# Cached key pages turned by VectorE in 32x32 blocks, and their scores as sixteen 32x32 tiles

## The chip, the cores and the metric

The kernel runs on one core of a Trainium2 chip. The metric is the device time of one execution in microseconds (us): the median of three runs.

## The reference

One inference step of a small two-layer decoder: 256 prompt tokens and 64 sample tokens (8 sequences of 8 new tokens), model width 1024. The first layer is a retention layer, then keys and values shared by the rest are computed, and the second layer is attention with 8 heads of width 128. For the sample tokens, attention also reads a paged cache: 8 sequences, 2 pages each, a page being 128 positions x 8 heads x 128. What the change touches is this part:

```
def moba_sample(q, k_new, v_new, cache_k, cache_v, page_table, rel_bias):
    ...
        k_past = cache_k[pages].reshape(past, MOBA_HEADS, MOBA_HD)
...
    s_sel = jnp.einsum('qhd,qhjld->qhjl', q, k_sel).astype(jnp.float32) + b_sel
...
    p = jax.nn.softmax(logits, axis=-1)
```

So for each sequence and head, 8 queries meet 256 cached keys over a width of 128, in float32, a bias is added, and a softmax over the cached and the own keys follows.

## The kernel before

Each engine has one in-order program, written out from a single list of steps that `make_schedule` (L128) lays down; the engines meet at semaphores only. TensorE's main work is the projections: a weight matrix is streamed in chunks of 1 MB. For each chunk the steps WS split it on ScalarE (`w_hi`, L1185) and VectorE (`w_lo`, L1523) into two parts, in four pieces, and TensorE makes three products per block (L881, L884, L865). Small steps of attention are hung between the tiles of a chunk, at numbered slots: six slots to a chunk of three tiles, one in the middle and one at the end of each tile.

The stretch that matters holds five such chunks. I call them K1, K2, K3, K4 (key projection: the two halves of the depth for the first 512 columns, then for the second) and V1 (the first half of the first value projection). Their slots are 0 to 29. After each tile of K2 and K4 the key rows are complete, and the step TILE normalises them: square on ScalarE (L1357), sum on VectorE (L1683), root on ScalarE (L1359), reciprocal (L1686) and four scalings on VectorE (L1692). The third tile first adds two halves (L1549).

Cached keys, before: SyncE loads page n (`load_page`, L665) into one of four buffers `cache`, 128 positions on the partitions. Step KP n turns it: eight 128x128 transposes on TensorE (L1048) into two PSUM banks, copied out to `ktc` by VectorE (L1815) and ScalarE (L1453). Step KS b (L1061), for one sequence, multiplies the two turned pages with that sequence's queries: eight matmuls 128x32 by 256, four of them in different column groups of the array, all into bank 5. The queries lie spread over zeros in `wide`, written by ScalarE in step ME (L1251). Step SE (L1824) adds the bias for the first four sequences, and step SA p does it for the others and takes the maximum (L1837 to L1850). KX turns the new keys (L1077), SN scores them (L1092), SB turns the weights of the softmax, PV multiplies them with value pages.

```
    for n in range(8):
        at = 2 + 3 * n
        if n:
            g[at].append(("KS", n - 1))
        if n == 4:
            g[at].append(("SE",))
        g[at] += [("KP", 2 * n), ("KP", 2 * n + 1)]
```

Each of VectorE, ScalarE, GpSimd and SyncE walks through the same list, so within a slot the order is: split pieces, then the steps of the middle slot, then TILE, then the steps of the end slot.

Of the kernel before, what the change touches and what calls it, by code (L numbers as in the profile page):

```python
# [33 lines left out]
P = 128  # L34
D = 1024
# [38 lines left out]
def shape_constants():  # L74
# [21 lines left out]
    own = np.arange(P)[:, None] % 32 // NEW == np.arange(4)[None, :]  # L96
# [11 lines left out]
def kp_banks(n):  # L108

    return (6, 7) if n % 2 else (3, 4)  # L110
# [17 lines left out]
def make_schedule():  # L128
# [48 lines left out]
    def add(*s):  # L177
# [4 lines left out]
        if s[0] == "KS" and s[1] % 4 == 0:  # L182
            fill(5, "PS", s[1] // 4)
        if s[0] == "KP":
            for b in kp_banks(s[1]):
                fill(b, *s)
# [61 lines left out]
    for n in range(8):  # L248
        at = 2 + 3 * n
        if n:  # L250
            g[at].append(("KS", n - 1))
        if n == 4:
            g[at].append(("SE",))
# [42 lines left out]
def build(nc, a):  # L296
# [3 lines left out]
    with ctx:  # L300
# [109 lines left out]
        spread = wide.ap().rearrange("p n (b x) -> p n b x", x=32)[:, :, :, 0:NEW]  # L410
# [3 lines left out]
        yf = flat_ktc[:, :, 2 * (TP + P):D]  # L414
        flat_sqs = mvp[:, 0, 0:4 * P]
        sqs = flat_sqs.rearrange("p (g h m) -> p g h m", g=2, m=32)
# [55 lines left out]
        wide_cleared, pads_cleared = sem("wide_cleared"), sem("pads_cleared")  # L472
        q_sq_done = sem("q_sq_done")
# [45 lines left out]
        def await_ks(eng, n):  # L519

            b = n // 2
            if n < 0:
                return
            if b % 4 == 3:
                await_full(eng, 5, "PS", b // 4)
            else:
                eng.wait_ge(ks_done, b + 1 - (b + 1) // 4)

        def window(n, bb):

            return wide[:, n, 24 * bb:24 * bb + 32]

# [90 lines left out]
        def _(sp):  # L623
# [41 lines left out]
            def load_page(n):  # L665

                m, vals = n % 16, n >= 16
# [5 lines left out]
                src = a["cache_v"] if vals else a["cache_k"]  # L673
                sp.dma_start(cache[:, n % NCP, :], src[bass.ds(page, 1)].rearrange("o p h d -> p (o h d)"))\
                    .then_inc(cache_loaded[n % NCP], 16)
# [19 lines left out]
            for step in steps:  # L695
# [74 lines left out]
                elif kind == "ME" and step[1] == 5:  # L770
                    sp.wait_ge(lines_stored, 64)
                    for h in range(MH):
                        r0 = 32 * (h % 4)
                        sp.dma_start(bs[r0:r0 + 32, h // 4, :],
                                     bass.AP(scratch.tensor, h * LINE + FAR - PAST, [[0, 4], [skew, NEW], [1, PAST + NEW]]))\
                            .then_inc(bias_loaded, 16)
# [34 lines left out]
        def _(pe):  # L811
# [83 lines left out]
            for step in steps:  # L895
# [145 lines left out]
                elif kind == "KP":  # L1041
                    n = step[1]
                    pe.wait_ge(cache_loaded[n % NCP], 16 * (n // NCP + 1))
                    for h in range(MH):
                        b = kp_banks(n)[h // 4]
                        if h % 4 == 0:
                            await_free(pe, b, *step)
                        mm = pe.transpose(bank[b][:, P * (h % 4):P * (h % 4) + P], cache[:, n % NCP, P * h:P * h + P], ident)  # L1048
                        if h % 4 == 3:
                            close(mm, b)  # L1050
                elif kind == "KS":
                    b = step[1]
                    for n in range(2 * b, 2 * b + 2):
                        for kp_bank in kp_banks(n):
                            await_read(pe, kp_bank, "KP", n)
# [954 lines left out]
```

## Time and profile before

| | before |
|---|---|
| median of 3 runs, us | 509.81 |
| lowest, highest | 509.31, 509.97 |
| span of the profiled execution, us | 508.2 |
| TensorE busy | 502.0 us, 99% |
| VectorE busy | 352.5 us, 69% |
| ScalarE busy | 263.2 us, 52% |
| GpSimd busy | 74.6 us, 15% |
| DMA | 125.49 MB, mean 247 GB/s |

The span runs from the first to the last instruction of one profiled execution. The profile states no total time for it besides the span; the median of the runs is 1.6 us above it. Busy shares are averages over the whole span; TensorE's matmuls are pipelined, so 99% says that it hardly waits, not that it works at its peak.

### The profile page before, as it was taken

To read this page: it belongs to the slowest core of one execution; us is meant where nothing else is said; L and a number is where in the kernel's file an instruction comes from. 1 tells how busy PE (TensorE), PEld (TensorE's weight loads), DVE (VectorE), ACT (ScalarE), POOL (GpSimd) and SP (SyncE) were. 2 spreads that over 40 slices of the span, in tenths; PEclk is the share of its full clock that TensorE was granted. 3 is DMA by queue.
4 is the path that set the end of the run, shared out by engine and by line. 5 is a ranking of instruction groups with operands and counts; after the bars stand their busy time and mean duration, and the time that the engine had idled before them with its cause. 6 is when DMAs were issued, how large, how long until landed. Compare 5 with 4: busy or idle time off the path is not lost.

```text
span 508.2 us, 9171 instructions
## 1 busy us (share of the span) xinstructions
PE 502.0 (99%) x3401; PEld 434.0 (85%) x3401; DVE 352.5 (69%) x651; ACT 263.2 (52%) x532; POOL 74.6 (15%) x85
## 2 busy tenths in 40 slices
PE   7999999999999999999999999999999999999997
PEld 6989978899779978898899999977877778999885
DVE  3865539884789829893598978836756765676662
ACT  5836532574428633464652556945444655655630
POOL 0291004520082102720000240000000000000000
PEclk9999999999999999999999999999999999999999
DMA  8993969999899898999937976526797657684211
GB/s 256 333 349 118 275 245 313 376 358 231 284 343 386 235 277 283 354 328 230 264 103 277 334 244 256 188 83 238 249 326 238 216 171 242 226 309 154 83 53 52
DMA packets 79375, 125.49 MB, mean 247 GB/s; under 512 B 4051, under 2 KB 42148, under 8 KB 79204
## 3 DMA queue, kind: packets, MB, share of 16 engines
q1 hardware_dynamic: 79250, 124.89, 75.4%
q8 instruction: 27, 0.44, 0.4%
q14 instruction: 16, 0.13, 0.1%
q10 hardware_dynamic: 82, 0.02, 0.0%
HBM read 98.93 MB, written 27.57 MB: 249 GB/s over the span
## 4 chain that ended last, share of the span: by engine, by line
PE 95%; DVE 2%; DMA 1%; ACT 1%; issue 1%; SPq 0%; DVEq 0%; ACTq 0%
PE bank L884 45%; PE bank L881 20%; PE bank L865 7%; PE bank L1048 3%; PE bank L993 3%; PE bank L1061 2%; PE bank L1115 1%; PE bank L1007 1%; PE bank L940 1%; PE bank L1161 1%; PE bank L820 1%; PE bank L973 1%; PE bank L974 1%; PE bank L975 1%; DMA eye<-in_c_eye 1%; PE bank L961 1%
## 5 line engine op out<-in xcount | busy, mean ns | idle before, releaser
L1523 DVE TENSOR_TENSOR w_lo<-w_raw,w_hi 128x512 fp32r<-128x512 f32 x207 | 143.8, 733 | 65.7 <-ACT w_hi L1185 65.2
L1185 ACT ACTIVATE w_hi<-w_raw 128x512 fp32r<-128x512 f32 x208 | 118.4, 620 | 58.3 <-PE bank L884 35.0
L884 PE MATMUL bank<-xn_hi,w_hi 128*128 128x320 f32 x320 | 100.1, 317 | 0.7 <-ACT w_hi L1185 0.7
L884 PE MATMUL bank<-xn_hi,w_lo 128*128 128x320 f32 x320 | 97.7, 309 | 0.1
L884 PE MATMUL bank<-xn_lo,w_hi 128*128 128x320 f32 x320 | 97.6, 309 | 0.0
L881 PE MATMUL bank<-w_hi,xn_hi 128*128 128x512 f32 x160 | 65.0, 406 | 0.0
L884 PEld LDWEIGHTS bank<-xn_hi,w_hi 128*128 128x128 f32 x320 | 59.7, 188 | 4.7 <-issue 2.9
L881 PE MATMUL bank<-w_lo,xn_hi 128*128 128x512 f32 x160 | 62.6, 391 | 0.0
L881 PE MATMUL bank<-w_hi,xn_lo 128*128 128x512 f32 x160 | 62.5, 390 | 0.0
L884 PE MATMUL bank<-ym_hi,w_hi 128*128 128x320 f32 x192 | 60.9, 317 | 0.0
L884 PEld LDWEIGHTS bank<-xn_lo,w_hi 128*128 128x128 f32 x320 | 59.8, 188 | 0.4 <-DVE xn_lo L1572 0.2
L884 PEld LDWEIGHTS bank<-xn_hi,w_lo 128*128 128x128 f32 x320 | 59.7, 188 | 0.3 <-DVE w_lo L1523 0.3
L884 PE MATMUL bank<-ym_hi,w_lo 128*128 128x320 f32 x192 | 59.3, 309 | 0.0
L884 PE MATMUL bank<-ym_lo,w_hi 128*128 128x320 f32 x192 | 59.3, 309 | 0.0
L1745 DVE SCALAR_TENSOR_TENSOR st<-st,bank 128x512 f32<-128x512 f32 x64 | 39.6, 680 | 6.2 <-PE bank L1007 6.2
L884 PEld LDWEIGHTS bank<-ym_hi,w_hi 128*128 128x128 f32 x192 | 36.1, 188 | 1.8 <-issue 1.7
L884 PEld LDWEIGHTS bank<-ym_lo,w_hi 128*128 128x128 f32 x192 | 36.1, 188 | 0.1
L881 PEld LDWEIGHTS bank<-w_hi,xn_hi 128*128 128x128 f32 x160 | 30.1, 188 | 7.2 <-issue 1.7
L884 PEld LDWEIGHTS bank<-ym_hi,w_lo 128*128 128x128 f32 x192 | 36.0, 188 | 0.0
L881 PEld LDWEIGHTS bank<-w_lo,xn_hi 128*128 128x128 f32 x160 | 30.0, 188 | 6.6
L881 PEld LDWEIGHTS bank<-w_hi,xn_lo 128*128 128x128 f32 x160 | 30.1, 188 | 5.4
L1941 POOL TENSOR_TENSOR fin<-raw_qk,cst 128x320 f32<-128x320 f32 x16 | 17.4, 1111 | 108.4 <-DMA out_ret_state_prompt<-fin 67.2
(265 smaller groups left out, 766.5 us busy)
## 6 DMA issues: line engine op xcount, KB each, us to landing
w_raw<-in_ret_w_in SPq DMA_DIRECT2D x23, 1024.0 KB, 10.8
st<-in_state_ret SPq DMA_DIRECT2D x32, 512.0 KB, 8.4
out_ret_state_sample<-st SPq DMA_DIRECT2D x32, 512.0 KB, 4.6
w_raw<-in_ret_w_out SPq DMA_DIRECT2D x8, 1024.0 KB, 8.8
w_raw<-in_moba_w_in SPq DMA_DIRECT2D x8, 1024.0 KB, 6.1
cache<-in_cache_k SPq DMA_DIRECT2D x16, 512.0 KB, 4.9
w_raw<-in_w_kv SPq DMA_DIRECT2D x8, 1024.0 KB, 6.4
cache<-in_cache_v SPq DMA_DIRECT2D x16, 512.0 KB, 4.0
```

The source lines that it names most:

```text
L820: mm = pe.transpose(bank[kt][:, c0:c0 + m], st[0:m, t, P * kt:P * kt + P], ident[0:m, 0:m])
L865: mm = pe.matmul(bank[b][:, :], xn_hi[:, k, TP:T + TS], w[:, wk, :], start=k == 0 and n == 0, stop=k == KT - 1 and n == 1)
L881: mm = pe.matmul(bank[b][0:m, :], x[:, k, c0:c0 + m], w[:, wk, :], **flags)
L884: mm = pe.matmul(bank[out][:, 0:T], w[:, wk, P * tile:P * tile + P], x[:, k, :], **flags)
L940: mm = pe.matmul(bank[5][0:m, col:col + n], kT[:, d, j:j + m], qT[:, d, i0:i0 + n], start=d == 0, stop=d == 1)
L993: mm = pe.matmul(bank[5][32 * j:32 * j + 32, :], qz[:, q0:q0 + 32], st[:, b, DV * d:DV * d + DV], start=False, stop=g == 1 and d == 1, ski ...
L1048: mm = pe.transpose(bank[b][:, P * (h % 4):P * (h % 4) + P], cache[:, n % NCP, P * h:P * h + P], ident)
L1061: mm = pe.matmul(bank[5][32 * j:32 * j + 32, PAST * half_at:PAST * half_at + PAST], window(2 * h + b // 4, b % 4), ktc[:, :, h, :], start= ...
L1185: act.activation(w_hi[:, c % 2, part], w_raw[:, c % RAW, part], ACT.Copy).then_inc(w_hi_done, 1)
L1523: dve.tensor_tensor(w_lo[:, c % 2, part], w_raw[:, c % RAW, part], w_hi[:, c % 2, part].bitcast(F32), ALU.subtract).then_inc(w_lo_done, 1)
L1745: dve.scalar_tensor_tensor(state, state, math.exp(NEW * LOG_DECAY[h]), bank[up_bank(b, d)][:, :], ALU.mult, ALU.add).then_inc(bank_read[up ...
L1941: done(pool.tensor_tensor(to, x, tab, ALU.mult))
```

## The change

- Key pages are loaded in another layout. Partition group g (32 partitions) of the page buffer holds heads 2g and 2g+1, with position 32c+i of the page on partition i of the group. That takes four DMAs to a page with runs of 256 numbers, in place of one with runs of 1024. The pages come in another order (`key_page`), four to a quad: two sequences.
- KP n is one VectorE instruction: it turns 32 blocks of 32x32 in each group of partitions (1024 elements on each partition), SBUF to SBUF, into `ktc` or the new `ktc2`. These two hold one quad; the next quad waits for the scores of the last. No TensorE or ScalarE work is left in KP.
- KS q, now four steps, multiplies a quad: 64 matmuls of a 32x32 tile of the array by 256 columns, over four blocks e of the head width, four partition groups (each into its own bank, 3 to 6) and four column groups. KP 0 to 15 stand in slots 0-3, 6-9, 12-15 and 18-21, KS 0 to 3 in slots 5, 11, 17 and 23.
- SE has two steps (slots 12 and 24), each with four instructions, since a score is now the sum of two banks. The instruction L1837 in SA falls away.
- `wide` is filled by GpSimd in ME, four small copies to a head, where ScalarE's one instruction (L1251) falls away. GpSimd also builds `own_q`, and clears part of `wide` after the last KS.
- SN has twice as many matmuls, and KX turns 128 rows where the last tile had 64. KX 0 and 1 move to slots 14 and 16. The bias loads are sixteen DMAs in place of eight.

```diff
+def key_page(n):
+
+    q, s, pg = n // 4, n % 4 // 2, n % 2
+    return NPG * (4 * (q // 2) + 2 * s + q % 2) + pg
...
-    for n in range(8):
-        at = 2 + 3 * n
...
-        g[at] += [("KP", 2 * n), ("KP", 2 * n + 1)]
-    g[16].append(("KX", 0))
-    g[18].append(("KX", 1))
-    g[26].append(("KS", 7))
+    for n, at in enumerate((0, 1, 2, 3, 6, 7, 8, 9, 12, 13, 14, 15, 18, 19, 20, 21)):
+        g[at].append(("KP", n))
+    for q, at in enumerate((5, 11, 17, 23)):
+        g[at].append(("KS", q))
+    g[12].append(("SE", 0))
+    g[24].append(("SE", 1))
+    g[14].append(("KX", 0))
+    g[16].append(("KX", 1))
...
                 elif n >= NCP:
-                    await_full(sp, kp_banks(n - NCP)[1], "KP", n - NCP)
+                    sp.wait_ge(kt_done, n - NCP + 1)
...
+                src = a["cache_k"][bass.ds(page, 1)].rearrange("o (c i) h d -> i (o c) (h d)", i=32)
+                for g in range(4):
+                    sp.dma_start(cache[32 * g:32 * g + 32, n % NCP, :].rearrange("p (c x) -> p c x", c=4), src[:, :, 256 * g:256 * g + 256])\
+                        .then_inc(cache_loaded[n % NCP], 16)
...
                 elif kind == "KS":
...
+                    q = step[1]
+                    pe.wait_ge(kt_done, 4 * q + 4)
+                    pe.wait_ge(wide_filled, MH)
+                    if q % 2 == 0:
+                        for b in PS_BANKS:
+                            await_free(pe, b, "PS", q // 2)
+                    last = {}
+                    for e in range(4):
+                        for s in range(2):
+                            at = 32 * (2 * s + q % 2) - NEW * (q % 2)
+                            for h in range(2):
+                                for g in range(4):
+                                    rows_at, c0 = slice(32 * g, 32 * g + 32), 32 * (2 * h + s)
+                                    keys_of = (ktc, ktc2)[s][rows_at, :, 4 * h + e, :]
+                                    last[g] = pe.matmul(bank[PS_BANKS[g]][c0:c0 + 32, 0:PAST], wide[rows_at, 8 * h + 2 * e + q // 2, at:at + 32],
+                                                        keys_of, start=q % 2 == 0 and e == 0, stop=q % 2 == 1 and e == 3,
+                                                        skip_group_check=True)
...
                 elif kind == "KP":
                     n = step[1]
-                    b = kp_banks(n)[0]
-                    await_full(dve, b, *step)
-                    await_ks(dve, n - 2)
-                    dve.tensor_copy(ktc[:, n % 2, 0:4, :], bank[b][:, :].rearrange("p (h k) -> p h k", h=4))\
-                        .then_inc(bank_read[b], 1)
+                    dve.wait_ge(cache_loaded[n % NCP], page_loaded(n))
+                    if n >= 4:
+                        await_ks(dve, n // 4 - 1)
+                    dve.transpose(keys_turned(n), cache[:, n % NCP, :].rearrange("p (c x j) -> p x c j", c=4, j=32)).then_inc(kt_done, 1)
...
                 elif kind == "SE":
...
+                    for x in range(2):
+                        for u in range(2):
+                            b, p = PS_BANKS[2 * u + x], 2 * half + u
+                            to = scores_at(p)[:, 0:PAST]
+                            dve.scalar_tensor_tensor(to, bank[b][:, 0:PAST], rsq[:, 16 + p:17 + p], to if x else bs[:, u, 0:PAST],
+                                                     ALU.mult, ALU.add).then_inc(bank_read[b], 1)
...
+            def spread_queries(h):
+
+                g, x = h // 2, h // 2 % 2
+                pool.wait_ge(q_done, h + 1)
+                for e in range(4):
+                    done.wait()
+                    ins = pool.tensor_copy(slots[32 * g:32 * g + 32, 8 * (h % 2) + 2 * e:8 * (h % 2) + 2 * e + 2, :, 16 * x:16 * x + NEW],
+                                           mqT[32 * e:32 * e + 32, h, TP:T].rearrange("p (n b t) -> p n b t", n=2, t=NEW))
```

## Rows read from the trace of the kernel before

**Rows 1.** The profile's page: busy time and share, and the clock by slices.

```profile
PE 502.0 (99%) x3401; PEld 434.0 (85%) x3401; DVE 352.5 (69%) x651; ACT 263.2 (52%) x532; POOL 74.6 (15%) x85
PEclk9999999999999999999999999999999999999999
```

**Rows 2.** The page's chain that ended last, by engine.

```profile
PE 95%; DVE 2%; DMA 1%; ACT 1%; issue 1%; SPq 0%; DVEq 0%; ACTq 0%
```

**Rows 3.** The chain in order of time, 334 to 396 us: start, length, what.

```profile
335.30 1.75 PE bank L1048 x16
...
341.60 1.00 PE bank L1061 x16
342.60 1.90 PE bank L1048 x16
344.50 4.11 PE bank L881 x18
...
390.93 0.85 PE bank L1077 x6
...
395.22 0.63 PE bank L1092 x32
```

**Rows 4.** Busy time by stretch: length; PE, PEld, DVE, ACT, POOL; clock, DMA share, GB/s.

```profile
335.10:395.20 60.10, 60.10 (x442) 45.51 (x444) 36.24 (x78) 27.73 (x56) 0.00 (x0) 1.00 0.72 246
```

**Rows 5.** VectorE's groups in that stretch: busy us, mean ns, idle before.

```profile
L1523 DVE TENSOR_TENSOR w_lo<-w_raw,w_hi 128x512 fp32r<-128x512 f32 x17 | 11.1, 683 | 6.0 <-ACT w_hi L1185 6.0
L1815 DVE COPY ktc<-bank 128x512 f32<-128x512 f32 x16 | 10.5, 682 | 4.5 <-PE bank L1048 4.3
```

**Rows 6.** VectorE's timeline: start us, us, instruction, and the idle time before.

```profile
345.69 1.29 DVE L1523 TENSOR_TENSOR w_lo<-w_raw,w_hi 128x512 fp32r<-128x512 f32 x2 [0.90 <-ACT w_hi L1185]
348.00 0.69 DVE L1683 TENSOR_REDUCE small<-scr 128x4 f32<-128x512 f32 x1 [1.02 <-ACT scr L1357]
349.27 1.13 DVE L1692 SCALAR_TENSOR_TENSOR rows<-bank,small,knw 128x128 f32<-128x128 f32 x4
350.31 0.68 DVE L1523 TENSOR_TENSOR w_lo<-w_raw,w_hi 128x512 fp32r<-128x512 f32 x1
...
356.48 0.67 DVE L1549 TENSOR_TENSOR rows<-bank,rows 64x512 f32<-64x512 f32 x1
357.85 0.68 DVE L1683 TENSOR_REDUCE small<-scr 64x4 f32<-64x512 f32 x1 [0.70 <-ACT scr L1357]
363.16 0.86 DVE L1824 SCALAR_TENSOR_TENSOR ps<-bank,small,bs 128x256 f32<-128x256 f32 x2
```

**Rows 7.** VectorE's groups of other shapes, whole execution; L1760: min/median/max ns.

```profile
L1787 DVE TENSOR_TENSOR scr<-scr,rsb 128x1280 f32<-128x1280 f32 x3 | 4.5, 1488 | 0.1
L1874 DVE TENSOR_SCALAR ktc<-ktc,small 128x256 f32<-128x256 f32 x8 | 2.8, 353 | 0.3
L1875 DVE TENSOR_SCALAR ktc<-ktc,small 128x128 f32<-128x128 f32 x8 | 2.2, 279 | 0.0
L1692 DVE SCALAR_TENSOR_TENSOR rows<-bank,small,knw 128x128 f32<-128x128 f32 x16 | 4.5, 344 | 0.1
L1760 DVE TENSOR_TENSOR scr<-scr x4: 825/1472/1483, 94.3 to 253.3; 128x640 f32<-128x640 f32 x4
```

**Rows 8.** TensorE's tiled matmuls in time: start us, us.

```profile
348.55 1.07 PE L1061 MATMUL bank<-ktc,wide 128*32 128x256 f32 x16
83.03 0.50 PE L1007 MATMUL bank<-vq,kq 32*128 32x512 f32 x4
395.15 0.65 PE L1092 MATMUL bank<-mkT,mqT 128*32 128x64 f32 x32
```

**Rows 9.** SyncE's DMA issues in time: start us, us of issuing, transfer.

```profile
366.04 0.55 SPq L789 DMA_DIRECT2D out_k_sample<-rows  x1
371.57 0.35 SPq L674 DMA_DIRECT2D cache<-in_cache_k  x1
```

**Rows 10.** GpSimd's group of 64-column operations: busy us, mean ns, idle before.

```profile
L1954 POOL TENSOR_TENSOR qz<-qT,cst 128x64 f32<-128x64 f32 x8 | 6.0, 760 | 0.0
```

More of the change, by code:

```diff
@@ L181, in add @@
             fill(5, "UR", s[1])
[L182 to L186, printed above, removed]
+        if s[0] == "KS" and s[1] % 2 == 0:
+            for b in PS_BANKS:
+                fill(b, "PS", s[1] // 2)
         if s[0] == "SB":
@@ L1040, in _ @@
                     close(mm, 7)
[L1041 to L1050, printed above, removed]
-                elif kind == "KS":
[L1052 to L1055, printed above, removed]
-                    if b % 4 == 0:
-                        await_free(pe, 5, "PS", b // 4)
-                    for half_at in range(2):
-                        for j in range(4):
-                            h = 4 * half_at + j
-                            mm = pe.matmul(bank[5][32 * j:32 * j + 32, PAST * half_at:PAST * half_at + PAST],
-                                           window(2 * h + b // 4, b % 4), ktc[:, :, h, :],
-                                           start=b % 4 == 0 and half_at == 0, stop=b % 4 == 3 and half_at == 1,
-                                           skip_group_check=True)
-                    if b % 4 == 3:
-                        close(mm, 5)
@@ L1067, in _ @@
                     else:
[L1068 removed]
+                        last[3].then_inc(ks_done, 1)
                 elif kind == "KX":
@@ L1073, in key_columns @@
                     def key_columns(i, t):
-                        c0, m = TOK[t]
+                        c0 = TOK[t][0]
                         at = 256 * (c % 2) + P * i
-                        return pe.transpose(bank[6 + i][:, c0:c0 + m], rows[0:m, t, at:at + P], ident[0:m, 0:m])
+                        return pe.transpose(bank[6 + i][:, c0:c0 + P], rows[:, t, at:at + P], ident)
+                    if c == 0:
+                        pe.wait_ge(pads_cleared, 1)
                     for i in range(2):
@@ L1820, in _ @@
                 elif kind == "SE":
-                    await_full(dve, 5, "PS", 0)
-                    dve.wait_ge(bias_loaded, 16 * MH)
-                    for u in range(2):
-                        ins = dve.scalar_tensor_tensor(ps[:, u, 0:PAST], bank[5][:, PAST * u:PAST * u + PAST],
-                                                       rsq[:, 16 + u:17 + u], bs[:, u, 0:PAST], ALU.mult, ALU.add)
-                    ins.then_inc(bank_read[5], 1)
+                    half = step[1]
+                    dve.wait_ge(bias_loaded, 32 * MH)
+                    for b in PS_BANKS:
+                        await_full(dve, b, "PS", half)
+                    for x in range(2):
+                        for u in range(2):
[3 more added lines that the diff above has]
+                                                     ALU.mult, ALU.add).then_inc(bank_read[b], 1)
+                        if x == 0:
+                            await_read(dve, PS_BANKS[0], "PS", half)
+                            await_read(dve, PS_BANKS[2], "PS", half)
                 elif kind == "SA":
```

147 lines of the change are left out of this document (83 added, 64 removed).

## The prediction

> **What bounds the kernel now.** I read the page first: TensorE is busy 99% of the span, at the full clock in every slice [rows 1], and the chain that ended last is 95% TensorE [rows 2]. So work taken from TensorE shortens the run, as long as the engine that takes it over keeps up. The chain in order of time shows what goes: eight blocks of sixteen page transposes between the projections' matmuls, 1.75 us the first and 1.90 us the others, and eight score blocks of 1.00 us [rows 3]. The busy times of this stretch, 335.1 to 395.2 us, show who has room: VectorE is busy 36.24 of 60.10 us, ScalarE 27.73, GpSimd not at all [rows 4]. VectorE's groups say what it does there, and its timeline in which order, which is what will count [rows 5, 6].
>
> **TensorE's own sum.** The transposes fall away: 1.75 + 7 x 1.90 = 15.05 us. Score blocks: a block before has 16 instructions of 256 columns, four column groups side by side, in 1.00 us [rows 3, 8]: four rounds of 0.215 us (256 columns, two cycles each at 2.4 GHz) and 0.14 us of entry and exit. Four row groups have run side by side too: four matmuls of 512 columns have starts within 0.01 us and all end within 0.50 us [rows 8]. Rows and columns split at once are in no row. At best sixteen tiles share a round: the 128 instructions of a quad take 8 x 0.215 + 0.14 = 1.86 us, say 1.9. At worst only four run at a time: 32 rounds, 7.0 us. Between these, the 32 small instructions of SN start within 0.58 us, so issuing one takes at most 18 ns [rows 8]; by that bound alone a block is 2.3 us. I take 1.9, since both splits alone have run at full width, and keep 7.0. So scores cost 4 x 1.9 = 7.6 us where they cost 8.0; SN doubles from 0.63 us [rows 3] to 1.3; KX stays near 0.75 a step (0.85 in its row [rows 3]). TensorE's sum is -15.05 - 0.4 + 0.7 = -14.8 us.
>
> The Trainium skill (TensorE: Matmul & the Clock Gate, Packing small matmuls) reports a gain of 10.6 times, not 16, for sixteen tiles; by it a block would be an estimated 8 x 0.215 x 16/10.6 + 0.14 = 2.7 us, and the sum of the run 1.6 us more, since two of the four blocks lie open. Four groups have lost only the 0.14 us a block here [rows 8], so the trace rather speaks for 1.9, but no row has sixteen.
>
> **VectorE's price for a page.** KP was a 0.60 us copy (two of 128x512 back to back take 1.27 to 1.29 us; one alone 0.68 [rows 5, 6]). It becomes one instruction of 1024 elements on each partition, and no row has a transpose. Nearest is the plain operation of 1280 elements, 1.488 us [rows 7]: 256 elements fewer at 0.96 GHz make 1.22 us, and behind another instruction, where some 0.08 us overlap, 1.14. Below: scalings of 256 and 128 elements differ by 74 ns, 0.58 ns an element [rows 7], which gives 0.72 us in a row. Above: an operation of 640 elements has taken 0.825 us and also 1.483 [rows 7], the latter 2.3 ns an element, so 2.3 us. I take 1.14, one element a cycle, as most rows of VectorE have it.
>
> The Trainium skill (VectorE: DVE Perf Modes, The three transpose paths) gives 311 ns for a 128x128 transpose; eight of those would be an estimated 2.5 us a page. But a plain 128x128 operation takes 344 ns here and 1280 elements 1488 [rows 7], so most of such a figure is fixed cost, paid once here.
>
> VectorE's sum in the stretch: 36.2 - 10.5 (copies) + 16 x 1.14 + 6 more bias instructions at 0.40, two of them moved from behind the stretch = 46.3 us, where TensorE needs 60.1 - 14.8 = 45.3. VectorE becomes at least as full as TensorE, and it waits inside its order. So I lay its order out.
>
> **The ledger.** t = 0 is the end of KS 0. TensorE reaches KS 0 1.75 us sooner, at 339.85; pages 0 to 3 follow VectorE's last pieces for K1 near 333.2 and end at 338.4, so nothing waits; t = 0 is 341.75. A tile's normalising T takes 2.31 us on VectorE (348.00 to 350.31) and can start 0.76 us after the tile [rows 6]; the third tile has 0.6 + 0.78 us more in front (356.48 to 357.85). A tile on TensorE takes 12 x 0.228 = 2.74 us, the third 1.82 (18 take 4.11 [rows 3]).
>
> *K2.* VectorE: page 4 from 0.1 to 1.2; then it stands until tile 0 is squared, 3.5; T to 5.8; page 5, 6.95; piece 7.55; page 6, 8.7; T 11.0; page 7, 12.1. KS 1 needs page 7. TensorE has been done with K2 since 7.3: **it stands 4.8 us**. KS 1 ends at 14.05.
>
> *K3.* VectorE: piece and third tile to 16.4, two pieces 17.6, page 8 18.7, SE 0 (four at 0.40) 20.4, page 9, piece, page 10, KX copy, page 11 24.8, piece, KX copy 25.85. TensorE: KX 0 uses bank 6, so it waits for SE 0 from 18.2 to 20.4; KX 1 for a copy 0.25 us; KS 2 for the last copy, 25.4 to 25.9: 2.9 us in all. KS 2 ends at 27.8.
>
> *K4* is K2 again: page 12 to 28.95, T from 31.3 to 33.6, page 13, piece, page 14, T, page 15, 39.9. TensorE is done at 35.1 and **stands 4.8 us**; KS 3 ends at 41.85.
>
> *V1.* VectorE: third tile to 44.2, two pieces, SE 1 to 47.1. TensorE: KX 2 at 46.0 waits for it 1.2 us; KX 3, SN; V1 ends at 53.2, which is 394.95. Before, it ended at 396.65 (SN's end 395.73 and four matmuls). Thus 14.8 us saved and about 13.1 given back: -1.7 us. Some fifteen handovers between engines that I set at zero or 0.05 us make it -1.4.
>
> **What I cost at nothing, and its cover.** *SyncE:* a page is four issues, at 0.55 us for a strided one against 0.35 for a plain one [rows 9], so 2.2 us for 0.35. Page n is asked for when page n-4 is turned and needed four pages later, 6 us or more; weight chunks queued behind it are asked for a whole chunk ahead. The bytes are the same, 246 GB/s at a DMA share of 0.72 before [rows 4]. If loads run at half speed since each lands on 32 partitions only, 12 us of the stretch's 55 go on top, and the queue fills; that is in the upper range. The eight more bias loads lie before 335 us. *GpSimd:* four copies a head at no more than 0.76 us [rows 10] are 3 us; the last head's end near 336.6 us, before 339.85; `own_q` and the clearing have tens of us. *ScalarE* only loses work, in a stretch where it is half idle.
>
> A measurement of this kernel can tell about 0.2%, 1.0 us, from no change.
>
> **Rivals.** (a) *The cover holds:* VectorE keeps ahead and all 14.8 us come off: 495.0. Against it: 46.3 us of busy time in 45.3, and in-order waits on top. Chance 0.03. (b) *Cheap transposes:* at 0.72 us each, ten of the sixteen pages on the path save 0.42 us: 508.4 - 4.2 = 504.2. The rows of scalings speak for it, all other rows against: 0.10. (c) *Dear transposes,* slower than before: at 2.2 us in a row, pages 5 to 7, 8 to 11, 13 to 15 each add 1.06 us and the first four 2.9: 508.4 + 13.5 = 522. It decides from 1.3 us a page: ten pages at 0.14 make up the gain. The 1.483 us row speaks for it: 0.13, mostly below its full price. (d) *Tiles don't run sixteen wide:* 7.0 us a block; KS 0 and 2 add 5.1 each, KS 1 and 3 have 3.5 us of slack behind them and add 1.6 each: 522. 0.07. (e) *The clock:* before, the row of clocks has no fallen slice, and TensorE never stood for long [rows 1]; now it stands 4.8 us twice, at 60 to 75% busy around it. If it falls to 1.2 GHz, KS 1 and KS 3 take 1.9 us more and the next tile up to 2.7; K3 hides all but 0.5 us behind SE 0, V1 all but 1.5: 510.5, and 512 or more if it stays down. 0.14. The Trainium skill (TensorE: Matmul & the Clock Gate, HAM oscillation) states that a TensorE which idles between bursts drops to half clock; no row here has it idle to show it. (f) *Nothing moves:* the stands give back all that the transposes leave, so that the work has only changed its engine: 509.8, 0.03.
>
> **The numbers.** The likeliest is the ledger, 0.50: 509.8 - 1.4 = 508.4 (span 506.8). Its own range is 506 to 510.8, since 0.1 us on a page's price is 1 us on the result: some 0.31 of it is faster by over 0.2%, 0.14 within, 0.05 slower. With (a), (b) that makes faster 0.45; with (f) and a mild (e) within 0.18; (c), (d) and most of (e) slower 0.37. The range leaves out (a), (d) and the dear end of (c): 503.5 to 517.
>
> **What would show it.** Right: VectorE's transposes, sixteen of about 1.2 us; TensorE standing before the second and the fourth score block, some 5 us each, and before the first and third turning of new keys, released by VectorE; score blocks of 1.9 us. Wrong: no standing (then (a) or (b)), a DMA as the releaser of a transpose, blocks over 2.5 us, or clock digits under 9 from 350 us on.

## The result: slower by 1.5%

The kernel after takes **517.44 us** (median of 4 runs, 516.87 to 518.44), the kernel before 509.77 (509.31 to 509.97) on the same chip: ratio 1.0151, 95% interval 1.0137 to 1.0165. Predicted were 508.4 us, and 517.0 at most. The profiled execution of after took 518.44 us, 516.7 of it span (before: 508.2).

The page of the profile after, and its chain by engine (compare [rows 1, 2]):

```profile
PE 495.1 (96%) x3689; PEld 427.3 (83%) x3689; DVE 362.6 (70%) x655; ACT 252.2 (49%) x508; POOL 87.9 (17%) x123
PE   8999999999999999999999999996776999999997
PEclk9999999999999999999999999997978999999999
...
PE 69%; DVE 16%; DMA 7%; issue 3%; ACT 2%; SPq 2%; POOL 0%; DVEq 0%; ACTq 0%; POOLq 0%
```

TensorE did lose work, 502.0 us of busy time against 495.1, though part of what is left runs at a lower clock. But it now stands in the stretch that was changed: slices 28 to 31. The stretches of after there, with the columns of [rows 4]:

```profile
335.10:340.30 5.20, 5.20 (x39) 3.63 (x37) 4.50 (x5) 1.01 (x2) 2.80 (x8) 1.00 0.44 123
340.30:343.10 2.80, 2.80 (x130) 1.92 (x130) 1.57 (x3) 1.62 (x5) 0.00 (x0) 1.00 0.78 208
343.10:355.50 12.40, 7.44 (x35) 5.82 (x35) 9.21 (x18) 3.43 (x7) 0.00 (x0) 0.93 0.96 238
355.50:360.00 4.50, 4.50 (x129) 2.72 (x129) 3.40 (x9) 2.49 (x5) 0.00 (x0) 0.50 1.10 257
360.00:369.30 9.30, 9.09 (x47) 7.33 (x48) 9.04 (x14) 1.52 (x4) 0.00 (x0) 0.97 0.88 221
369.30:377.60 8.30, 3.72 (x129) 2.01 (x129) 1.29 (x2) 1.03 (x2) 0.00 (x0) 0.79 1.03 293
377.60:391.50 13.90, 9.06 (x32) 7.05 (x32) 9.15 (x18) 3.42 (x7) 0.00 (x0) 0.87 0.78 202
391.50:395.70 4.20, 4.16 (x129) 2.76 (x130) 3.10 (x9) 2.27 (x5) 0.00 (x0) 0.63 0.94 300
395.70:405.70 10.00, 10.00 (x109) 8.20 (x110) 6.13 (x14) 3.05 (x6) 1.04 (x2) 1.00 0.66 226
```

Rows 2, 4, 6 and 8 of it are the four score blocks: 2.7, 4.5, 8.3 and 4.1 us long, where 1.9 each was predicted. V1 ends at 405.70; before it ended at 396.65: 9.05 us later, of which 8.5 are left in the two spans and 7.7 in the medians. The same in the chain in order of time (as [rows 3]):

```profile
340.36 2.69 PE bank L1079 x118
343.04 2.96 PE bank L904 x12
...
354.19 1.24 DVE scr L1829
...
367.02 1.15 DVE scr L1829
...
369.29 2.61 PE bank L1079 x101
371.90 4.58 issue
376.48 1.11 PE bank L1079 x16
377.59 4.56 PE bank L904 x12
...
390.25 1.25 DVE scr L1829
391.54 4.08 PE bank L1079 x127
395.62 4.32 PE bank L904 x18
```

Two things stand out. DVE L1829, the page turn, is where it was expected to be, last ahead of the second and the fourth block. And inside the third block TensorE stops for 4.58 us with "issue" as its only entry, that is, waiting for nothing that the profile shows. The block's last sixteen matmuls and the next tile come behind the stop at a lower clock (0.50 and 0.63 on the mean): 4.56 us for a tile that takes 2.74.

Against the ledger's times, the differences grow so:

```
event         ledger   measured  difference  what was added since the line above
KS 0 ends     341.75   343.04      +1.3      0.5 before it, 0.8: the block is longer than 1.9
KS 1 starts   353.85   355.48      +1.6      0.3
KS 1 ends     355.80   359.94      +4.1      2.5: 0.8 for its size, 1.8 for half clock
KS 2 starts   367.65   369.29      +1.6     -2.5: VectorE's order hides it
KS 2 ends     369.55   377.59      +8.0      6.4: 4.6 stop, 0.8 size, 1.0 half clock
KS 3 starts   381.70   391.54      +9.8      1.8: K4's first tile at half clock
KS 3 ends     383.60   395.62     +12.0      2.2: 0.8 for its size, 1.4 for the clock
V1 ends       394.95   405.70     +10.8     -1.3: room in V1
```

"Size" is what a block takes at full clock, 2.69 us, over the predicted 1.9; "clock" is what it took beyond 2.69.

### The profile page after: what moved, and what is told of

Same layout as the page of the kernel before. It is cut to its first block, busy times and chain, and to the rows that moved or that the text cites. A ratio compares the mean times of both kernels' runs of the same rounds, so it can differ in the third digit from the quotient of the medians.

```text
span 516.7 us, 9892 instructions
## 1 busy us (share of the span) xinstructions
PE 495.1 (96%) x3689; PEld 427.3 (83%) x3689; DVE 362.6 (70%) x655; ACT 252.2 (49%) x508; POOL 87.9 (17%) x123
## 4 chain that ended last, share of the span: by engine, by line
PE 69%; DVE 16%; DMA 7%; issue 3%; ACT 2%; SPq 2%; POOL 0%; DVEq 0%; ACTq 0%; POOLq 0%
PE bank L907 34%; PE bank L904 15%; PE bank L888 5%; DVE w_lo L1537 5%; DMA w_raw<-in_ret_w_in 3%; DMA w_raw<-in_ret_w_out 3%; DVE st L1759 3%; PE bank L1079 2%; PE bank L1138 2%; DVE scr L1829 1%; PE bank L1016 1%; DVE ktc L1829 1%; PE bank L1184 1%; DMA v_rows<-vs_split 1%; DVE scr L1795 1%
## 6 DMA issues: line engine op xcount, KB each, us to landing
w_raw<-in_ret_w_in SPq DMA_DIRECT2D x23, 1024.0 KB, 10.8
```

## Experiments

All are measured against the kernel before on the same chip (its medians there: 509.6 to 510.3). Where a heading says "cut", the kernel leaves work out or turns the wrong blocks, as its expectation says: its outputs are not right, and only its time is of use. A "stand" is a stretch in which TensorE waits for another engine; the "stop" is the 4.58 us above.

**e1, pages first.** Is it the order of VectorE's queue?

```diff
-    for n, at in enumerate((0, 1, 2, 3, 6, 7, 8, 9, 12, 13, 14, 15, 18, 19, 20, 21)):
+    for n, at in enumerate((0, 1, 2, 3, 6, 6, 6, 6, 12, 12, 12, 12, 18, 18, 18, 18)):
```

> The changed kernel, with the four page turns of K2, K3 and K4 all at the first slot of their chunk, ahead of the tile normalisings. Order theory (VectorE's in-order program puts two normalisings of 2.3 us between the pages, and TensorE stands 5 us before the second and fourth score block): both stands shrink under 1 us, the clock stays full there, the score blocks that took 4.46 and 4.08 us take 2.7; with VectorE as the bound of the stretch the time falls by 8 to 12 us, to 506 to 509. Rival, instruction supply (the 4.58 us stop inside the third score block is TensorE waiting for its own instructions): that stop stays, also with full clock, and the time falls by no more than 6 us. Rival, VectorE's sum of work alone is the cause: under 3 us.

520.10 us, ratio 1.0189 (1.0157 to 1.0222), where 506 to 509 was expected. The stand before the second block shrank to 2.9 us and the one before the fourth went, and both blocks ran at full clock. But others came: the stop is still there (3.41 us), and TensorE stands 8.9 us before the first turning of new keys. Its chain has a page load as a piece, and then four page turns with SE 0 behind them:

```profile
346.09 5.16 DMA cache<-in_cache_k
...
365.38 2.32 DVE scr L1829 x2
367.70 0.77 DVE ps L1842 x2
```

The edit moves more than it names: in slot 12 all four turns now stand ahead of SE 0 (L1842), for which that turning of keys waits. So the 8.9 us are not the loads alone.

**e2, TensorE kept busy in the stands,** by two bursts of six idle matmuls in each.

```diff
+                    if q % 2:
+                        ...
+                        for more in (2, 3):
+                            pe.wait_ge(kt_done, 4 * q + more)
+                            for _ in range(6):
+                                pe.matmul(bank[7][:, 0:T], xn_hi[:, 0, 0:P], xn_hi[:, 0, 0:T], start=True, stop=True)
```

> The changed kernel, with two bursts of six idle matmuls (0.9 us each) inside each of the two stands, into a bank that nobody reads then. Clock theory: no stretch of half clock after the stands, score blocks 2 and 4 fall from 4.46 and 4.08 us to 2.7; the third block does not hang on a stand of 5 us, so its stop stays. K3 and V1 hide part of the gain, so the time falls by 0.5 to 3 us. Rival, the clock costs nothing since VectorE hides it: within 0.5 us. Rival, the clock falls for another reason: digits and block times as before.

518.27 us, ratio 1.0142 (1.01 to 1.0185): nothing that can be measured. The second block became 3.97 us instead of 4.46, the fourth stayed at 4.06 us (391.20 to 395.26), and the stop in the third was 5.00 us. Bursts of 1.1 us did not hold the clock: 0.5 us of each stand was left between them and 2.3 us behind the second. The chain now waited for a page (357.44, 8.60 us) ahead of the third block. So this run does not price the clock.

**e3, a quarter of the score matmuls (cut).**

```diff
-                    for e in range(4):
+                    for e in range(1):
```

> The changed kernel, with the score blocks over the first quarter of the head width only: 16 of 64 matmuls each, 32 instructions in place of 128. Instruction supply: a block takes 0.7 us, the stop of 4.58 us inside the third block is gone, and so is the half clock in K4's first tile; with 2.0 us less in each of the four blocks (two of them open) the time falls by 9 to 12 us. Rival, the stop has another cause (a semaphore, a DMA): a stop of 3 us or more stays and the time falls by 3 to 5 us. Order theory: the two stands before blocks 2 and 4 stay at 4.5 to 5.5 us in either case.

513.14 us, ratio 1.0054 (1.0035 to 1.0072): 4.3 us less than after, where 9 to 12 was expected, and no stop in the third block. But the stands before the second and fourth block grew to 8.0 and 9.0 us, because page loads land late. Its waits of TensorE, and two pieces of its chain:

```profile
PE bank L1079 <- DVE scr L1829: 17.0, 2, 9.0
```
```profile
346.00 9.03 DMA cache<-in_cache_k
...
378.13 9.44 DMA cache<-in_cache_k
```

So the many small instructions, with the stop, cost at least 4.3 us, and the loads stand right behind.

**e4, the kernel before with one page transpose in four (cut).** What was there to win?

```diff
-                        mm = pe.transpose(bank[b][...], cache[...], ident)
                         if h % 4 == 3:
-                            close(mm, b)
+                            close(pe.transpose(bank[b][...], cache[...], ident), b)
```

> The kernel before, with one page transpose in four: 96 of 128 are left out, so three heads in four are scored against old contents; all copies, waits and loads stay. If TensorE is the bound of that stretch and the others can follow: 96 x 0.119 = 11.4 us less, 498.4. If VectorE, ScalarE or the page loads are close behind: 3 to 8 us less, and the chain shows who releases TensorE.

502.34 us, ratio 0.9852 (0.9823 to 0.9881), 7.3 us less, where 96 transposes at 0.119 us (1.90 us for sixteen [rows 3]) are 11.4. Even with everything else in place a third of the gain is lost to waits: VectorE, ScalarE and TensorE normalise the key tiles in turns (chain: `L1691`, `L1548`, `L1814` between matmuls).

**e5, e6, e7: plain page loads (cut),** alone, with the pages first, and with each score block in four parts as well.

```diff
-                for g in range(4):
-                    sp.dma_start(cache[32 * g:32 * g + 32, n % NCP, :].rearrange("p (c x) -> p c x", c=4), src[:, :, 256 * g:256 * g + 256])\
+                sp.dma_start(cache[:, n % NCP, :], a["cache_k"][bass.ds(page, 1)].rearrange("o p h d -> p (o h d)"))\
...
```

> The changed kernel, with each key page loaded by one DMA of 128 rows as before, so that the turned blocks are of the wrong heads and positions; same bytes, one issue for four. Theory that the four-part loads are the next limit but hidden here behind VectorE's order: the time falls by less than 1.5 us, the two stands stay near 5 us, pages land within 5 us of their issue where parts took up to 9.8. Theory that crowded DMA engines delay TensorE's instruction fetch: the stop in the third score block shortens by 1 us or more. Rival, the loads cost nothing anywhere: no difference over 0.5 us.

> Plain loads and the page turns at the first slot of each chunk. Order theory: with the pages there in time, no stand before score blocks 2 and 4 (under 1 us), full clock in both, VectorE hardly idle in the stretch; 506 to 511. Rival, page loads still come too late with plain loads too: VectorE waits for a cache DMA and the time is 514 or more, as with parts (520.1). The stop in the third block stays, 3 to 5 us, in either case.

> As plain loads with pages first, and each score block cut into four parts of 32 instructions at separate slots. Instruction supply theory: no stop of over 1 us in any score part, and full clock; 3 to 5 us less than the same kernel with whole blocks. Rival, the stop hangs on that place in time (a burst of other DMAs) and not on the density of instructions: a stop of 3 us or more remains.

517.92 (ratio 1.0179, 1.0146 to 1.0212), 516.21 (1.0127, 1.0107 to 1.0147) and 517.84 us (1.0171, 1.0143 to 1.02). In the kernel after the loads cost nothing by themselves: e5 has the same stands and stop. (The stop did not shorten either: 4.85 us, at a DMA share of 1.06.) The waits of TensorE in e5, 335 to 410 us:

```profile
PE bank L1077 <- DVE scr L1827: 9.8, 2, 5.0
PE bank L1077 <- issue: 4.9, 1, 4.9
```

With the pages first, even plain loads landed 9 us after their issue (e6: 339.45, 8.97 us), which I put down to the four page buffers coming free together; e6 keeps a stop of 3.45 us and the 8.9 us before the first turning of new keys, where SE 0 stands behind four turns as in e1. e7 shows no stop of "issue" inside a block, but stands of 3.0, 7.1, 0.9 and 2.6 us on VectorE, and it is not faster than e6, where 3 to 5 us less was expected.

**e8 (cut) and e11: the kernel before with four transfers a page,** in the form of the kernel after (e8) and as four times 32 whole rows (e11).

```diff
+                    for g in range(4):
+                        sp.dma_start(cache[32 * g:32 * g + 32, n % NCP, :].rearrange("p (c x) -> p c x", c=4), src[:, :, 256 * g:256 * g + 256])\
```
```diff
+                    for g in range(4):
+                        sp.dma_start(cache[32 * g:32 * g + 32, n % NCP, :],
+                                     a["cache_k"][bass.ds(page, 1)].rearrange("o p h d -> p (o h d)")[32 * g:32 * g + 32, :])\
```

> The kernel before, with each key page loaded in the four parts of the change, so that heads and positions are mixed up; nothing else moves. If the four-part loads and their issues are too slow for this stretch: TensorE waits for pages and the time rises by 2 to 8 us. If the path has room: within 1 us, and parts land later than the 4.9 us of a page before without anybody waiting.

> The kernel before, with each key page loaded by four transfers of 32 whole rows (4 KB a row) in place of one of 128 rows: as many transfers and waits as in the kernel before with the loads of the kernel after (520.4), but the layout in memory stays the plain one. If SyncE's issues are what cost 10.8 us there, it is 516 or more. If it is the form of the transfer (1 KB pieces gathered from all 128 rows for 32 partitions), it is 509.5 to 511.5, and the issues cost 0.35 to 0.5 us each without being waited for.

e8: **520.41 us**, ratio 1.0206 (1.0183 to 1.023). e11: 512.22, ratio 1.0037 (1.0015 to 1.006). So in the kernel before the form of the loads costs 10.8 us, and of that the four issues and transfers cost 1.9. The stretch 335 to 400 us of before, e11, e8:

```profile
335.00:400.00 65.00, 65.00 (x492) 49.38 (x491) 40.63 (x89) 31.70 (x64) 0.00 (x0) 1.00 0.74 255
```
```profile
335.00:400.00 65.00, 63.79 (x484) 48.33 (x483) 39.24 (x85) 29.84 (x60) 0.00 (x0) 1.00 0.85 249
```
```profile
335.00:400.00 65.00, 56.43 (x400) 43.20 (x399) 35.85 (x76) 26.46 (x52) 0.00 (x0) 0.95 0.92 229
```

Read the last two columns: the share of the DMA engines rises from 0.74 to 0.92 while the rate falls from 255 to 229 GB/s. Share over rate rises by 38% in e8 and by 18% in e11, for all the bytes of the stretch, weights included. Both fill 32 partitions with each transfer, so the step from 18% to 38%, and from 1.9 to 10.8 us, is that from whole rows of 4 KB to 1 KB pieces. TensorE waits 8.6 us for pages in e8.

**e10b (and e10): the instruction stream moved.** A "fetch" is one of the profile's instruction transfers on queue q8, 16 KB each. Tiny matmuls, 64 in e10 and 32 in e10b, ahead of the turning of the queries in K1.

```diff
+                    for _ in range(32):
+                        pe.matmul(bank[7][0:32, 0:1], ident[0:32, 0:32], ident[0:32, 0:1], start=True, stop=True)
```

> The kernel after, with 64 tiny 32x32 matmuls of one column (128 instructions more, results overwritten) on TensorE before the turning of the queries, in the first key chunk; nothing else differs. They cost 1 to 1.5 us there. Instruction-supply theory: the 4.58 us stop inside the third score block comes because a fetch of TensorE's instructions falls into the block; half a fetch more ahead of it moves the place of the fetch, so the stop is gone from the third block or sits at another instruction, or in another block (the second or fourth, where VectorE is waited for anyway): 512 to 515 if it is gone, 518 to 519 if it moves to another open place. Rival, something bound to the third block (a bank, the data, VectorE): the stop stays after the same 101 matmuls, and the time is 518.5 to 519.

> The run with 64 tiny matmuls kept the stop at the same 102nd matmul of the third block; each tiny matmul is two matmuls and two weight loads in the trace, so 256 instructions were added, which is one whole fetch of 16 KB (64 bytes each), and the trace has one fetch more. So it could not move the place of the fetch. Now 32 tiny matmuls, 128 instructions, half a fetch. Instruction-supply theory: the stop is not at the 102nd matmul of the third block; it is gone or stands in the middle of another block or tile. Rival, something bound to the third block: it stays at the 102nd. Time: the tiny matmuls cost some 2 us (4.1 us for 64); 514 to 516 if the stop is gone, 519 to 521 if it is anywhere on the path.

e10: 524.37 us, ratio 1.0273 (1.0248 to 1.0299); the stop is 4.85 us long, again behind the 102nd matmul of the third block. It had been meant as half a fetch and was a whole one, as the expectation of e10b says, so by that theory the stop had to stay where it was. The tiny matmuls took 4.1 us, and the first block behind them 3.98 us. e10b: 518.00 us, ratio 1.0134 (1.0108 to 1.0159), and **the stop is gone from the third block**. Parts of the block in TensorE's timeline of after, and of e10b:

```profile
371.05 0.85 PE L1079 MATMUL bank<-ktc,wide 32*32 32x256 f32 x13
376.48 1.11 PE L1079 MATMUL bank<-scr,wide 32*32 32x256 f32 x16 [4.58 <-issue]
```
```profile
374.61 0.64 PE L1081 MATMUL bank<-ktc,wide 32*32 32x256 f32 x8
...
375.10 0.49 PE L1081 MATMUL bank<-scr,wide 32*32 32x256 f32 x8
375.52 0.50 PE L904 MATMUL bank<-w_hi,xn_hi 128*128 128x512 f32 x1
```

In after, a fetch runs inside the stop. The DMA view of 373.8 to 375.1 us:

```profile
DMA packets 364, 0.50 MB, mean 383 GB/s; under 512 B 47, under 2 KB 209, under 8 KB 363
q1 hardware_dynamic: 363, 0.48, 101.5%
q8 instruction: 1, 0.02, 5.1%
```

And of 255.9 to 257.5 us, where the fetch has the engines to itself and TensorE is busy throughout:

```profile
q8 instruction: 1, 0.02, 4.2%
```

Of 1.3 us and 16 engines, 5.1% is 1.06 us for these 16 KB, while all engines are full with page and weight data; the lone one took 1.08 us. So the transfer itself is not slowed. It is late: between the starts of the fetches at 357.70 and 373.94 TensorE began 426 matmuls and weight loads, and only 51 more until the next, where the mean over the run is some 250. TensorE goes on 1.5 us after the fetch's end, and that is the rule here: all ten stops of over 0.6 us that the profiles put down to "issue" (after, e1, e2, e5, e6, e9b, e10, e12b, e13, e14) end 1.3 to 1.6 us after the end of a fetch. The whole execution has 29 fetches, before had 27; in e10b they lie at 365.71 and 378.00, on either side of the third block.

But the time did not fall. The tiny matmuls took 2.1 us, and behind them the first block ran at a clock of 0.60, in 4.01 us, though TensorE had not stood. And the stand before the fourth block became 8.0 us, behind a page:

```profile
380.39 9.38 DMA cache<-in_cache_k
389.80 1.25 DVE scr L1831
391.10 4.08 PE bank L1081 x127
```

**e9b: cheap turns (cut), and e12b: weight pieces on GpSimd.** Two ways to relieve VectorE alone.

```diff
-                    dve.transpose(keys_turned(n), cache[...].rearrange("p (c x j) -> p x c j", c=4, j=32))
+                    x = 8 if n < 4 else 2
+                    dve.transpose(keys_turned(n)[:, 0:x, :], cache[...].rearrange("p (c x j) -> p x c j", c=4, j=32)[:, 0:x, :, :])
```
```diff
+                if kind == "WS" and step[1] in lo_by_pool:
+                    ...
+                    pool.tensor_tensor(w_lo[:, c % 2, part], w_raw[:, c % RAW, part], w_hi[:, c % 2, part].bitcast(F32), ALU.subtract)
```

> The kernel after, with VectorE's last twelve page transposes cut to a quarter (two of eight column groups; the rest of these turned pages keeps what the first four pages left there, every wait and every load stays). VectorE's price theory: an instruction falls from 1.15 us to some 0.35, so 0.8 us goes for each of some ten pages on the path, 8 us, and with shorter stands the clock may stay up, another 0 to 4: 505.5 to 509.5. Load theory (the page loads, four transfers to 32 partitions each, are what the stretch waits for once VectorE is quicker, as in the run with a quarter of the scores): the chain passes page loads of 9 us, and the time stays above 512. The stop inside the third block should stay in both, as its instructions are the same.

> The kernel after, with the sixteen w_lo pieces of the second to fourth key chunks and of the first value chunk on GpSimd in place of VectorE; same arithmetic. GpSimd took 1.30 us for such a piece, VectorE 0.57 to 0.68. Theory that VectorE's in-order sum sets the stands: some 9.5 us leave VectorE; two pieces lie ahead of the last page in the second and in the fourth chunk, three or four in the third and behind it, so 0.6 us each for eight of them: 5 us less, 511.5 to 514. Rival: GpSimd's and VectorE's operations slow each other, or the loads bound the stretch (as with the pages first): 516 to 519.

e9b: 514.83 us, ratio 1.0087 (1.0056 to 1.0119): 2.6 us less than after, not 8. e12b: 517.73, ratio 1.0122 (1.0088 to 1.0156): nothing clear of the noise. Both did shorten the stands before the second and fourth block, from 4.96 and 4.88 us to 2.56 and 2.44 (e9b), and to 4.36 and 4.28 (e12b). And both got a page load ahead of the third block in return:

```profile
357.78 8.07 DMA cache<-in_cache_k
365.87 0.45 DVE scr L1830
...
370.05 4.03 issue
```
```profile
360.32 8.68 DMA cache<-in_cache_k
369.02 1.25 DVE scr L1836
```

**e13 and e14: limits lifted together (cut).** e13 is e9b, plain loads and the shift of e10b in one; e14 leaves VectorE's turns whole.

> The kernel after with all three suspects out of the way: key pages loaded by one plain transfer each (so the blocks that are turned are not the right ones), VectorE's last twelve turns cut to a quarter, and the instruction stream moved by half a fetch (32 tiny matmuls, some 2 us). Theory of three limits close to each other (VectorE's order, the page loads, the stop), each of which hides what lifting another one gives: alone they gave 0 (loads), 2.6 (turns), 0 (stop); together 7 to 10 us: 507 to 511. Rival: something else keeps the stretch long (clock, handovers): 513 or more.

> The kernel after with plain page loads (blocks not the right ones) and the stream moved by half a fetch; VectorE's work whole. In the run with the shift alone the stop was gone, but the stand before the fourth block grew from 4.9 to 8.0 us behind a page load of 9.4 us. Three-limits theory: with plain loads that stand is 4.9 us again, so 3 us less than 518.0: 514.5 to 515.5. Rival (the time lost at the stop comes back somewhere whatever the loads do): 517 to 518.

e13: **510.05 us**, ratio 0.9995 (0.9978 to 1.0013): 7.4 us less than after, where the single steps gave 0, 2.6 and 0. (It still has a stop, 0.84 us in K2's first tile.) Cheap turns with only one of the other two were not run, so which of them the rest hangs on is open. e14: 517.53, ratio 1.0136 (1.0108 to 1.0164), where 514.5 to 515.5 was expected: a miss. The waits of TensorE in e14 say why:

```profile
PE bank L1079 <- DVE scr L1829: 9.8, 2, 5.0
PE bank L902 <- issue: 2.2, 1, 2.2
```

The stand before the fourth block is back at 4.9 us, as expected. But TensorE stopped in another place, right behind the first block, in K2's first tile (345.92 to 348.07), and that tile too went on at a lower clock. TensorE's program is the same as in e10b, which has no stop there; only the loads differ. So the stop does not only follow the stream, it also depends on the loads.

**e15 and e16: the four transfers cut the other way,** each 256 columns of all 128 partitions; e16 adds GpSimd's pieces and the shift, and is a whole kernel.

```diff
-                src = a["cache_k"][bass.ds(page, 1)].rearrange("o (c i) h d -> i (o c) (h d)", i=32)
-                for g in range(4):
-                    sp.dma_start(cache[32 * g:32 * g + 32, n % NCP, :].rearrange("p (c x) -> p c x", c=4), src[:, :, 256 * g:256 * g + 256])\
+                src = a["cache_k"][bass.ds(page, 1)].rearrange("o (c i) (g h) d -> g (o c) i (h d)", i=32, g=4)
+                for c in range(4):
+                    sp.dma_start(cache[:, n % NCP, 256 * c:256 * c + 256], src[:, c])\
```

> The kernel after with the same bytes to the same places, but the four transfers of a page cut the other way: each fills 256 columns of all 128 partitions (1 KB pieces) in place of 1024 columns of 32 partitions. If few partitions make the landing slow, pages land in 5 us or less where they took up to 9.8, and the DMA share falls. If the 1 KB pieces make it slow, landing and share stay. The time itself stays at 516.5 to 517.8 either way, since VectorE and the stop hold it there.

> A whole kernel with every output: the kernel after with the wide form of the page loads, sixteen weight pieces on GpSimd, and the stream moved by half a fetch. If the wide loads land sooner, VectorE's 4 to 5 us and the stop's 4.6 us count together, less 2 us for the tiny matmuls: 509.5 to 512. If loads land as before, the chain passes them and it stays at 514 to 517. Beating the kernel before would need more than all three give by my sum.

563.18 us (ratio 1.1054, 1.102 to 1.1089) and 564.31 (1.1052, 1.1026 to 1.1078). Both theories fell: this form is by far the worst. 335 to 400 us of e15:

```profile
335.00:400.00 65.00, 30.89 (x364) 22.40 (x362) 28.46 (x48) 13.67 (x30) 3.72 (x11) 0.73 0.40 121
```

Only 0.40 of the DMA engines' time is used, at 121 GB/s, and SyncE takes 1.16 us for an issue (median) in place of 0.32. Share and rate fall together, so the engines are not full. From 362 to 374 us, where TensorE does nothing, the share is 0.28 at 92 GB/s, near a quarter of sixteen engines; the outermost count of the source's pattern is 4 in this form and 32 in the other. That a transfer keeps only four engines busy here fits both numbers, but no run tried another count. No run gave a version that beats the kernel before.

## Why the prediction was wrong, point by point

*TensorE's sum, -14.8 us.* Right for what is removed. The score block was mis-sized: 2.69 us, not 1.9, which is 2.4 us on the three open blocks (the second one's share was hidden). The limit was in [rows 8] already: 32 small instructions in 0.58 us, 18 ns each, for which the prediction gave 2.3 us, and the last one's own 0.37 us comes on top; the estimate by the Trainium skill's 10.6 times (TensorE: Matmul & the Clock Gate, Packing small matmuls) was 2.7, and the trace agrees with it. I had called 1.9 nearer since both splits had run at full width; but at full clock the cost looks like issuing (starts some 17 ns apart through most of the block), which no wide instruction shows. That reading is argued from the starts; no run varied the columns.

*VectorE's price,* 1.14 us in a row and 1.22 alone: right, sixteen of these.

```profile
L1829 DVE STREAM_TRANSPOSE ktc<-cache x8: 1205/1236/1245, 333.7 to 385.1; 128x1024 f32<-128x1024 f32 x8
L1829 DVE STREAM_TRANSPOSE scr<-cache x8: 1204/1236/1237, 336.5 to 390.3; 128x1024 f32<-128x1024 f32 x8
```

e9b's quarter turns took 0.44 us, so an element costs (1236 - 440) / 768 = 1.04 ns, as taken. Rivals (b) and (c) are out. (The 311 ns from which the prediction estimated 2.5 us a page by the Trainium skill (VectorE: DVE Perf Modes, The three transpose paths) are given there for bf16; the float32 turns here took half of that estimate.)

*The stands.* Right: 4.96 and 4.88 us, where the ledger has 4.8 twice, released by VectorE's page turn:

```profile
PE bank L1079 <- DVE scr L1829: 9.8, 2, 5.0
PE bank L1079 <- issue: 4.6, 1, 4.6
```

The small stands before KX 0 and KX 2 did not come, since TensorE was late itself.

*The clock,* rival (e) at 0.14, came, and stood in a rival instead of in the ledger. Behind the stands of 4.9 us the granted clock was 0.50 through the second block, which is 1.2 GHz, and 0.63 on the mean of the fourth, so a block of 2.7 us took 4.46 and 4.08: 1.8 and 1.4 us more, where (e) had 1.9 each. For the two falls that it foresaw its price was not too low; K3 hid all of the first (VectorE's order gave back 2.5). What it lacks is the third fall, behind the stop: 2.8 us. Here the rows show the clock down after stands of 4.9 and the stop of 4.6 us; before KS 2, where TensorE stood for only 0.2 us, the block began at full speed. By the Trainium skill (the same page as above, HAM oscillation) a TensorE that idles between bursts drops to half clock, and this trace agrees. Shorter stands went both ways: after 2.28 us (e2), 2.56 (e9b, second block) and 2.49 (e13, fourth) the block ran at a clock of about 0.6; after 2.87 (e1), 2.44 (e9b, fourth) and 2.56 (e13, second) at 1.00.

*The stop in the third block* is the step that failed most: the prediction has no term for the supply of TensorE's instructions, which is to put it at nothing, and gives no reason. It cost 4.58 us, and some 2.8 more from the half clock behind it (1.0 in the block, 8.30 - 2.69 - 4.58, and 1.8 in the next tile). I counted instructions only by what they take on the engine. A score block is 256 of TensorE's instructions in 2.7 us, one for every 10 ns, where a tile before was 24 in 2.7 us. Shown: with a quarter of them (e3) it is gone; moved by half a fetch (e10b) it leaves the block; moved by a whole one (e10) it is at the same matmul; and each of the ten stops ends 1.3 to 1.6 us after a fetch. Not shown is why the fetch is late. Its own 1.06 us are no longer than in an empty queue, so full queues could only hold it up before it starts, which the profile does not show. In seven of the ten stops the share of the DMA engines was 1.05 to 1.09, but in the three others 0.79 (e6), 0.36 (e14) and 0.01 (e13, the shortest).

*Page loads, costed at nothing.* In the kernel after that holds to the letter (e5: 517.92), and it is misleading: their lateness lies just under VectorE's and appears as soon as that is relieved (e3, e9b, e12b, e10b). "If loads run at half speed, 12 us on top" was the right size for the kernel before (e8: 10.8 us). The argument "the bytes are the same" was the error; 1 KB pieces take more of the queues than whole rows (38% against 18% in the stretch).

*The verdict.* With the terms measured, the ledger closes: 0.5 before KS 0, 0.8 for its block, 0.3, then 2.5, -2.5, 6.4, 1.8, 2.2 and -1.3 are 10.7 of the 10.8 us at V1's end; predicted 1.7 us gained there, measured 9.05 lost. By cause: the stop and the clock behind it 7.4, the size of the three open blocks 2.4, the clock in the fourth block 1.4, the rest -0.5. Nor did a repair of one term save it: the single steps gave at most 2.6 us (e3, which leaves out three quarters of the scores as well, 4.3). e13, with a quarter of VectorE's turns, plain loads and a moved stream, only comes level with the kernel before, of which 2.1 us are the tiny matmuls themselves, and its first and last block still take 4.01 and 4.07 us at a clock of 0.60 and 0.58, where its third takes 2.69 at full clock: 1.3 and 1.4 us for the clock. What stays open is which two of the three limits matter most together, and why the fetch comes late.

## What to carry to other kernels

When TensorE is 99% busy and work leaves it, the next limits can be within a few us of each other: here VectorE's order, the landing of the pages, the supply of instructions and the clock. Lay out each as a ledger of its own before adding up a gain, and test them by lifting two or three at once, since one at a time showed 0, 2.6 and 0 us here where all three together gave 7.4. Splitting a matmul into sixteen small tiles multiplies instructions: price it by the engine's issue rate and by instructions per us, not by columns. A load whose pieces get smaller is not the same load, even where the bytes are the same.

## What the runs showed of the hardware

- In or right behind a dense block TensorE stopped with nothing but "issue" to wait for: 4.6 to 5.0 us (after, e2, e5, e10, e12b), 4.0 (e9b), 3.4 and 3.5 with the pages first (e1, e6), 2.2 and 0.8 in K2 (e14, e13). Every stop ended 1.3 to 1.6 us after a 16 KB instruction transfer. Its place follows the stream: moved by half a fetch it left the third block. Such a transfer took 1.06 us at a DMA share of 1.05, and 1.08 us alone.
- 32x32 tiles in float32: 128 matmuls in 2.69 us, some 17 ns from start to start through most of a block, and 4.0 to 4.5 us behind stands of 4.3 us and more. 64 calls of a matmul with one column took 4.1 us, 32 took 2.1: each call is two matmuls, so 32 ns from start to start, though there is less to do than with 256 columns. The clock fell behind them (0.60 in the block that follows).
- Page loads as four transfers, each to 32 partitions in 1 KB pieces: 38% more DMA share per byte in the stretch, 10.8 us on the kernel before; as four times 32 whole rows 18% and 1.9 us; as four times 128 partitions by 1 KB, with 4 as the outermost count of the source, 121 GB/s and 563 us.
- VectorE's block transpose in float32: 1.236 us for 128x1024, 0.440 for 128x256. GpSimd's subtraction of 128x512 beside it: 1.28 us, no slower than alone (1.30).
